# Weight pieces of 1 MB: one 8 KB run per partition instead of two of 4 KB, with transposes that read every second column

## The reference: what is computed

```python
def clamped_swiglu(gate, up):
    gate = jnp.minimum(gate, SWIGLU_LIMIT)
    up = jnp.clip(up, -SWIGLU_LIMIT, SWIGLU_LIMIT)
    return gate * jax.nn.sigmoid(SWIGLU_ALPHA * gate) * (up + 1.0)
...
    def expert_block(args):
        xe, e = args
        h = clamped_swiglu(xe @ w_gate[e] + b_gate[e], xe @ w_up[e] + b_up[e])
        return h @ w_down[e] + b_down[e]
```

## Time and profile before

| | us |
|---|---|
| median of three runs | 1581.6 (1581.38 to 1587.18) |
| the profiled execution, whole | 1589.82 |
| its span, first to last instruction | 1587.9 |

### The profile page before, as it was taken

The page is one execution under the profiler, slowest core; times in us unless marked ns, Lnnn a source line. Parts: engine busy times, 40 slices in busy tenths (PEclk is TensorE's granted clock), DMA queues, the critical chain, the costliest instruction groups (busy, mean ns, idle before and its releaser), DMA issues.

```text
span 1587.9 us, 38738 instructions
## 1 busy us (share of the span) xinstructions
PE 1481.0 (93%) x17456; PEld 1027.5 (65%) x17456; DVE 382.9 (24%) x608; ACT 319.4 (20%) x585; POOL 113.7 (7%) x123
## 2 busy tenths in 40 slices
PE   6999699879669999999999999999999999999992
PEld 6777699567556666666666666666666666666661
DVE  2413664542641111111111111111111111111013
ACT  4424332121121111112111112111112111112113
POOL 2002000000010000001000000000000000000100
PEclk8999555669669999999999999999999999999996
DMA  9323000030879999999999999999999999999994
GB/s 299 118 70 96 0 1 0 4 113 1 324 262 399 373 392 383 392 391 392 387 390 384 393 385 390 376 385 379 384 389 376 386 380 378 379 391 386 384 349 134
DMA packets 128630, 468.27 MB, mean 295 GB/s; under 512 B 11408, under 2 KB 12672, under 8 KB 128320
## 3 DMA queue, kind: packets, MB, share of 16 engines
q1 hardware_dynamic: 117648, 429.01, 69.8%
q0 software_dynamic: 10832, 36.89, 9.0%
HBM read 445.19 MB, written 22.76 MB: 295 GB/s over the span
## 4 chain that ended last, share of the span: by engine, by line
PE 83%; PEld 6%; issue 3%; DVE 3%; ACT 2%; DMA 2%; PEldq 0%; DVEq 0%; SPq 0%; ACTq 0%; POOLq 0%
PE unit L989 38%; PE unit L992 25%; PE unit L809 3%; PEld unit L644 2%; PEld unit L646 2%; PEld unit L645 2%; PE unit L972 2%; PE unit L977 2%; PE unit L1006 1%; PE unit L796 1%; PE unit L773 1%; PE unit L644 1%; PE unit L942 1%; PE unit L646 1%; PE unit L645 1%
## 5 line engine op out<-in xcount | busy, mean ns | idle before, releaser
L992 PE MATMUL unit<-ring_a,xeT 128*32 128x256 f32 x1632 | 362.2, 380 | 0.0
L989 PE MATMUL unit<-ring_a,xeT 128*32 128x512 f32 (+1 forms) x3264 | 361.3, 487 | 0.0
L992 PE MATMUL unit<-ring_b,xeT 128*32 128x256 f32 x1440 | 318.6, 379 | 0.0
L989 PE MATMUL unit<-ring_b,xeT 128*32 128x256 f32 (+1 forms) x2880 | 317.8, 486 | 0.0
L992 PEld LDWEIGHTS unit<-ring_a,xeT 128*32 128x32 f32 x1632 | 178.6, 110 | 58.0 <-issue 0.5
L992 PEld LDWEIGHTS unit<-ring_b,xeT 128*32 128x32 f32 x1440 | 157.0, 110 | 50.9
L992 PE MATMUL unit<-ring_b,heT 128*32 128x256 f32 x816 | 179.1, 379 | 0.0
L989 PE MATMUL unit<-ring_b,heT 128*32 128x512 f32 (+1 forms) x1632 | 178.7, 486 | 0.0
L989 PEld LDWEIGHTS unit<-ring_a,xeT 128*32 128x32 f32 x3264 | 127.3, 110 | 68.0 <-issue 3.8
L989 PEld LDWEIGHTS unit<-ring_b,xeT 128*32 128x32 f32 x2880 | 111.1, 110 | 60.3 <-issue 2.5
L992 PE MATMUL unit<-ring_a,heT 128*32 128x256 f32 x672 | 147.3, 379 | 0.0
(11 more groups left out here) (303 smaller groups left out, 1647.2 us busy)
## 6 DMA issues: line engine op xcount, KB each, us to landing
ring_b<-w_down_dram SPq DMA_DIRECT2D x72, 1024.0 KB, 19.1
ring_a<-w_gate_dram SPq DMA_DIRECT2D x68, 1024.0 KB, 18.9
ring_a<-w_up_dram SPq DMA_DIRECT2D x68, 1024.0 KB, 20.7
ring_b<-w_gate_dram SPq DMA_DIRECT2D x60, 1024.0 KB, 19.4
ring_b<-w_up_dram SPq DMA_DIRECT2D x60, 1024.0 KB, 20.3
ring_a<-w_down_dram SPq DMA_DIRECT2D x56, 1024.0 KB, 19.4
raw_a<-w_in_dram SPq DMA_DIRECT2D x16, 512.0 KB, 5.0
raw_a<-w_out_dram SPq DMA_DIRECT2D x8, 512.0 KB, 3.7
```

Of the source, the lines that this page charges most:

```text
L989: return mm(out[j * NS:(j + 1) * NS, a:b], stat(j), w[:, a:b], start=False, stop=last)
L992: return mm(out[CAP:P, j * 256:(j + 1) * 256], stat(j), w[:, FOLD:D], start=False, stop=stop)
```

## The change

The rows of a piece are dealt to the partitions in another order: partition `p` takes rows `2p` and `2p + 1` of the 256, which are neighbours in HBM, so that its share is one run of 8 KB. Half `k` of a slot then holds the rows of parity `k`. The transposes follow: block `k` takes, of the 256 columns of its pair of blocks, every second one (`of_pairs`). The number of instructions, their order and their sizes on TensorE are unchanged, and biases, products, ring and waits stay as they are. A rarely used path for experts with over 96 tokens, which does not run on these inputs, keeps the old order with its own buffer.

```diff
-                        w = src[0, e, c * 256:(c + 1) * 256].rearrange("(k p) f -> p k f", p=P)
+                        w = src[0, e, c * 256:(c + 1) * 256].rearrange("(p k) f -> p k f", p=P)
                     else:
-                        w = src[0, bass.ds(e, 1), c * 256:(c + 1) * 256].rearrange("a (k p) f -> p (a k) f", p=P)
+                        w = src[0, bass.ds(e, 1), c * 256:(c + 1) * 256].rearrange("a (p k) f -> p (a k) f", p=P)
...
+            def of_pairs(src, k):
+                return src[:, k // 2 * 256:(k // 2 + 1) * 256].rearrange("s (p k) -> s k p", k=2)[:, k % 2]
+
             def x_T():
                 for k in range(KD):
-                    ins = tr(px[:, k * P:k * P + CAP], xg[:CAP, k * P:(k + 1) * P], ident[:CAP, :CAP])
+                    ins = tr(px[:, k * P:k * P + CAP], of_pairs(xg[:CAP], k), ident[:CAP, :CAP])
                 ins.then_inc(xT_done, 1)
...
             def h_T():
                 for k in range(FOLD // P):
-                    ins = tr(px[:, k * P:(k + 1) * P], hb[:, k * P:(k + 1) * P], ident)
+                    ins = tr(px[:, k * P:(k + 1) * P], of_pairs(hb[:], k), ident)
                 ins.then_inc(hT_done, 1)
```

## The result

The changed kernel takes 1595.98 us (median, 1594.26 to 1600.95) against 1581.62 us before in the runs beside it. The ratio is 1.0093, with a 95% interval of 1.0068 to 1.0117, or 14 us more. The forecast was no change, with a range to 1595. It was wrong. What came is rival A: the load took the 0.12 us that A named, and A's time was 1594 us. The range took in A at that price, and the median lies 1 us beyond its edge.

What follows compares the result with a forecast made beforehand. It took TensorE as the bound, by columns streamed, at 34.12 us per expert. Transfers and transposes summed to 0 + 0 against the profiled 1589.82 us; carried to the median, that gave 1581.6 us, range 1576 to 1595.

Steps and rivals of the forecast that it cites:

- rival A: In x_T and h_T: the strided load takes 0.12 us, 34.50 us per expert, 1594 us in all; chance 10%.
- What bounds the kernel: Expert stage: TensorE sets the pace by columns streamed, 34.12 us per expert, and weight pieces arrive in time.
- Part 1, the transfers: Weight pieces on the DMA engines: 8 KB runs gain 0 to 3%, worth 0 us because TensorE waits for none.
- The threshold: Weight transfers: at most 0.4% slower, 35.24 us per expert against 35.11; past it each further percent costs 9.8 us.
- The gathers: GpSimd's gathers share the DMA engines and may wait behind longer packets; 11 us to spare, so 0 us.
- Part 2, the transposes: x_T and h_T on TensorE read their stationary operand at a step of 8 bytes; taken as 0 us.
- The bound "twice as long": Strided load at 0.12 us: x_T grows by 0.28 us and h_T by 0.10, 12 us for 32 experts.
- the lower end: Transposes on TensorE: the strided load costs the same as the contiguous one, 0.06 us, so 0 us.
- cover: Time by which a transpose's load is hidden behind the matmuls' pace: 0.02 us in x_T, 0.05 in h_T.
- Rival B: Weight transfers: 8 KB runs carry 1.5% less, TensorE stands 11 us in the last quarter, 1593 us; chance 8%.
- Rival C: Weight transfers: unprofiled runs stall for pieces and the change gives that back, 1573 us; chance 4%.
- Rival D: DMA queue: every run is cut at 4 KB again, packets stay 117,648, 1581.6 us; within the forecast's 78%.

## Why the prediction was wrong, point by point

- **What bounds the kernel: right.** TensorE sets a beat of 34.12 us, transfers don't. The step and the runs taken alone show it from both sides.
- **Part 1, the transfers: right, in sign and size.** A saving of 2% lay within 0 to 3%, and it was worth 0. The threshold, 8 KB runs over 0.4% slower, was not reached; half a ring turns the same 2% into 14 us. The gathers, now behind longer packets, were not seen on the path.
- **Part 2, the transposes: wrong, and this is the step that failed.** The term that was mis-sized is the strided load. The text put it at 0.06 us, unchanged; it is 0.12. The bound "twice as long" and what follows from it, 0.38 us per expert and 12 us in all, are nearly what was measured, 0.43 and 13.3. The small rest is mostly in x_T (0.32 for 0.28). The text counted only the steps between loads, but the load by itself grew as well, the first of x_T from 0.14 to 0.20 us.
- **Why the choice inside the bounds was wrong.** The text took the lower end by the nearest loads, but no load in the trace had a step, so no row was near. What it called room, 0.02 us of cover in x_T, is a quarter of the matmul's 0.083. With an unknown rate on TensorE's own path and so thin a cover, a doubling should have had a far greater chance than 10%. That the time came within 1 us of the range is no merit of the forecast: the range reached so far only to take in rivals A and B.
- **The rules.** The Trainium skill, "Advanced Engine Details and Errata", section "SBUF Cachelines", counts two hits in 16 bytes as enough for full rate. By that a step of 8 bytes is free, and one of 16 is not. The measurement disagrees for TensorE's stationary operand: a step of 8 costs 0.12 us a load where contiguous loads follow in 0.06, and going on to 16 costs hardly more (x_T 1.15 us for 1.13). The Trainium skill, "TensorE: Matmul & The Clock Gate", section "LDWEIGHTS", gives 107 ns for 128 columns; contiguous loads here followed each other in 60 ns with no matmul ahead and in 83 behind the matmuls of x_T, strided ones in 120, so the figure lies between the two.
- **Rival B** did not occur: 8 KB runs alone, 1.0006. **Rival C** neither: the 8 us between the profiled execution and the median are no stall for pieces. In the profile of the long runs alone, x_T stands at 503.95 us where it was 510.66 in the kernel before, and the span is 1581.2 instead of 1587.9 us: all 6.7 us lie ahead of that point. The first x_T of all is already 6.8 us earlier (454.17 for 460.95), and the granted clock from 300 to 400 us is 0.91 where it was 0.81. **Rival D** fell with the packet count.
- **A slip in the description:** the section on the kernel says that ring_a has slots 0 to 11. It has 0 to 7, and ring_b 8 to 15. No number rests on it.

## What to carry to other kernels

A change that helps a resource off the critical path is worth what that resource was making others wait, which was 0; its side effects on the path are not discounted in the same way. When a layout change asks some operand to be read with a step, put the step on an engine with time to spare (VectorE here, where the new order costs 0.7 us per expert, hidden) and not on TensorE's stationary operand. And where the trace has no row for an access pattern on the bound engine, do not take the nearest row for it: a doubling of its price deserves a real chance.

## What the runs showed of the hardware

- Loads of a stationary fp32 operand of 128 columns follow each other every 0.12 us when it is read with a step of 8 bytes. Contiguous ones followed in 0.06 us with no matmul ahead, and in 0.083 or 0.11 us at the pace of the matmuls. A step of 16 bytes costs as much as one of 8 (x_T 1.15 and 1.13 us).
- The same step on a moving operand of 512 columns costs about 0.03 us a pass.
- Weight traffic in runs of 8 KB takes 34.4 us per expert, and in runs of 4 KB 34.9 to 35.1 us, so long runs save some 2%.
- A VectorE operation on 768 fp32 columns that reads PSUM contiguously and writes by turns to two places 1536 bytes apart takes 1.55 us instead of 0.96. One that writes contiguously and reads its second operand with a step of 8 bytes takes 1.06.
